# A fp32 decoder trunk in three-product arithmetic: the order of the first norm's halves, the place of the last closing's turn, and the order of products in the merge projection

## The chip, the cores and the metric

One core of a Trainium2 chip runs the whole program. The metric is device time in microseconds, the median over timed runs. The engines are TensorE (PE, with its weight loads as PEld), VectorE (DVE), ScalarE (ACT), GpSimd (POOL) and SyncE (SP), whose queue issues the large loads.

## The reference, cut to what matters

Two layers, x of 256 tokens by 1024 features, everything in float32:

```python
for l in range(2):
    h = rmsnorm(x, norm_mix[l])
    q_a, k_a, v_a, q_b, k_b, v_b, z, xbc, dt_raw = split_cols(h @ w_in[l], IN_SIZES)
    y_a = swa_sink_attention(rope(q_a), rope(k_a), v_a, sinks)      # 8 heads of 64
    y_b = moba_attention(q_b, k_b, v_b)                              # 8 heads of 64
    y_c = ssd_mixer(z, xbc, dt_raw, ...)                             # 16 heads of 64, chunks of 128
    g_a, g_b, g_c = split(sigmoid(h @ w_gate[l] + b_gate[l]), 3)
    merged = g_a * (y_a @ w_br_swa[l]) + g_b * (y_b @ w_br_moba[l]) + g_c * (y_c @ w_br_ssd[l])
    x = x + merged @ w_mix_out[l]
    x = x + cross_attention(rmsnorm(x, norm_cross[l]), rmsnorm(mem, norm_mem[l]))
    x = x + square(relu(rmsnorm(x, norm_mlp[l]) @ w_up[l])) @ w_down[l]
return rmsnorm(x, final_norm)
```

## The kernel before, in words

**Units.** The weights of a layer are cut into 93 units of up to 1 MB, numbered by the order in which PE takes them. A unit is 4 row tiles by 512 columns ("B": tokens on the output's partitions, two token tiles one after the other) or 8 row tiles by 256 columns ("A": output columns on the partitions, two column tiles m = 0 and 1). Each weight is used as a rounded high part and a low part, `w_hi` and `w_lo`, and each activation likewise; a product is three matmuls: high by high, high by low, low by high. An A unit is 48 matmuls, 24 in each half m. Units 0 and 1 are the first projection (`qa`), 2 is `qkb`, 3 to 5 are `kva`, 6 is `xbc`, 33 to 36 the last four gate units, 37 to 40 the third branch's projection `branch_c` (`w_br_ssd`; `U_BRC` is 37), 41 to 44 `mix` (`w_mix_out`; `U_MIX` is 41), 45 to 48 `kx`.

**The ring.** `raw`, `w_hi` and `w_lo` have three slots. SP loads unit u into `raw` when the low part of unit u - 3 has been made. ACT makes the high part (`hi`, line 751) after the load has landed and PE is through with unit u - 3; DVE makes the low part (`lo`, line 1468), and PE waits for that. ACT and DVE run `hi(u + 3)` and `lo(u + 3)` in the part of their program that belongs to unit u, in order with all else that they do.

**The order of other work.** All engines walk the same list of units; what belongs to a unit's slot stands in each engine's loop body. On PE, "inner" work is put between the two halves of a unit (`inner`), "outer" work behind the unit. SP's queue has one more stop: ahead of the load of unit 38 it waits for the end of the last of the third branch's products (`ssd_y`, 4), issues the 1 MB load of `mem` into the memory that `z_sb` used, and then the load of unit 38 (lines 589 to 591, and 641).

**The closings.** A closing ends a part of an attention or scan branch: DVE makes `y_tok` (line 1848 is the last step for the scan), PE turns it by four transposes into a PSUM bank (`close_turn`, line 1335), ACT reads the bank and makes the high part (`close_hi_part`, line 902), DVE reads it and makes the low part (`close_lo_part`, line 1862). There are eight, 0 to 7. Closing 7 holds the second token tile of group 1, that is the row tiles k = 4 to 7 of the operand `y_ssd` of `branch_c`. Its DVE part belongs to unit 34. Inner closings have `close_hi_part` at the head of ACT's body for their slot; outer ones have it a few lines further down in the body, but still ahead of `evacuate` and `hi(l, u + 3)`. Both kinds have it at their own slot:

```python
for i in INNER_CLOSINGS:
    if u == TURN_SLOT[i]:
        close_hi_part(l, i)
...
if u + RING < NU and w["kind"] != "xbc":
    hi(l, u + RING)
```

**The first norm.** `norm` keys ("norm", 0, b) are four PSUM banks: b = 2 t + u for token tile t and the k half of unit u. PE turns `h_tok` into them (`norm0_turn`, line 1189), ACT makes the high part of the activation (`norm_gain_hi`, line 781), DVE the low part (line 1489). Units 0 and 1 are multiplied in `opening`. Their weights are cut into halves of 1024 columns of a slot (`hi_half` line 760, `lo_half` line 1605), with signals of their own.

**Merged.** The merged activation is made in four parts (`mg_hi` by ACT, line 856, `mg_lo` by DVE, line 1759). Between units 41 and 42 PE does 16 transposes of `mem` (`norm_turn`, line 1208).

**The xs turn.** In slot 23 PE turns xs group 1 into the banks 7 (token tile 0) and 4 (token tile 1); DVE reads each with two products (`xs_tokens`, lines 1893 and 1895). Bank 7 is the one that PE's next turn of probabilities (line 1294) goes to.

Of the kernel before, what the change touches and what calls it, by code (L numbers as in the profile page):

```python
# [39 lines left out]
TT = SEQ // P  # L40
# [106 lines left out]
U_GATE, U_BRA, U_BRB, U_BRC, U_MIX = (first_of(k) for k in ("gate", "branch_a", "branch_b", "branch_c", "mix"))  # L147
# [44 lines left out]
CLOSINGS = [(3, 0, 0, 0), (7, 0, 1, 0), (11, 1, 0, 0), (15, 1, 1, 0),  # L192
            (17, 2, 0, 0), (19, 2, 0, 1), (21, 2, 1, 0), (23, 2, 1, 1)]
CLOSE_SLOT = [job_slot(c[0]) + 2 for c in CLOSINGS]
INNER_CLOSINGS, OUTER_CLOSINGS = (0, 1, 2, 6), (3, 4, 5, 7)
TURN_SLOT = [s + (3 if i == 1 else 2 if i in INNER_CLOSINGS else 1) for i, s in enumerate(CLOSE_SLOT)]

INNER_SLOTS = (ACS_SLOT, BTOK_SLOT, CB_SLOT) + XS_SLOTS + tuple(TURN_SLOT[i] for i in INNER_CLOSINGS)
# [120 lines left out]
def trunk(nc, a, out):  # L319
    ctx = ExitStack()  # L320
    with ctx:
# [113 lines left out]
        def sem(name):  # L435
            return ctx.enter_context(nc.semaphore(name))
# [66 lines left out]
        pool_steps = Signal(sem("pool_steps"), 9)  # L503
        sq_fin, ms_fin, rstd_fin = sem("sq_fin"), sem("ms_fin"), sem("rstd_fin")
        gain_ready, gained, fin_upper = sem("gain_ready"), sem("gained"), sem("fin_upper")

        def bank(key):
            return psum[:, BANK_OF[key][0], :]
# [10 lines left out]
        def is_read(l, key):  # L519

            b, k = BANK_OF[key]
            return bank_free[b], l * BANK_USES[b] + (k + 2)
# [214 lines left out]
        def _(act):  # L737
# [185 lines left out]
            def start(l):  # L923

                x_left(act, l, 0)
                square(0, 0, x_sb, sq_done.sem)
                if l == 0:
                    x_left(act, l, 1)
                    square(0, 1, x_sb, sq_done.sem)
                hi_half(l, 0, 0)  # L930
                if l == 0:
                    act.wait_ge(mix_cols, 1)
                    norm_gain_hi(l, 0, (0,))
                    hi_half(l, 0, 1)
                    norm_gain_hi(l, 0, (1,))
                    hi_half(l, 1, 0)
                    norm_gain_hi(l, 0, (2,))
                    hi_half(l, 1, 1)
                    norm_gain_hi(l, 0, (3,))
                    hi(l, 2)  # L940
                else:
                    hi_half(l, 0, 1)
                    norm_gain_hi(l, 0, (0, 1))
                    hi_half(l, 1, 0)
                    hi_half(l, 1, 1)
                    x_left(act, l, 1)
                    square(0, 1, x_sb, sq_done.sem)
                    hi(l, 2)
                    norm_gain_hi(l, 0, (2, 3))
# [97 lines left out]
        def _(pe):  # L1047
# [19 lines left out]
            def operand_ready(l, u):  # L1067

                w = UNITS[u]
                act, j = w["act"], w["index"]  # L1070
                if act == "relu":
                    pe.wait_ge(*relu_l.at(l, 2 * (j // 2) + 2))
                elif act == "merged":
                    pe.wait_ge(*mg_lo.at(l, 2 if w["first"] else 4))
                elif u > 0 and UNITS[u - 1]["act"] == act and (u != U_CO + 1):
                    return
                elif act == "mem":
                    wait_read(pe, l, [("norm", 1, b) for b in range(4)])
                elif act in ("h", "hq", "hf"):
                    return  # L1080
                elif act == "o":
                    wait_read(pe, l, [("xvalues", h) for h in ((0, 1) if w["first"] else (2, 3))])
                else:
                    pe.wait_ge(*is_read(l, ("closeT", {"y_swa": 1, "y_moba": 3, "y_ssd": 7}[act])))

            def unit(l, u, tiles=range(TT)):
                w, slot = UNITS[u], u % RING
# [30 lines left out]
                elif w["orient"] == "A":  # L1118
                    for m in range(n // P):
                        if m == 1:  # L1120
                            inner(l, u)
                        dst = bank(unit_banks(u, w)[m // 2])[:, (m % 2) * SEQ:(m % 2 + 1) * SEQ]
                        for k in range(kt):
                            if turned and m == 0 and k % 2 == 0:
                                pe.wait_ge(*is_read(l, ("norm", turned, k // 2)))
                            cs = slice(m * P, (m + 1) * P)
                            pe.matmul(dst, m_hi[:, k, cs], a_hi[:, k, :], start=k == 0, stop=False)  # L1127
                            pe.matmul(dst, m_hi[:, k, cs], a_lo[:, k, :], start=False, stop=False)  # L1128
                            ins = pe.matmul(dst, m_lo[:, k, cs], a_hi[:, k, :], start=False, stop=k == kt - 1)  # L1129
                else:  # L1130
                    for t in tiles:
                        if t == 1:
                            inner(l, u)
                        dst = bank(unit_bank(u, t))[:, 0:n]
                        for k in range(kt):
                            first, last = w["first"] and k == 0, w["last"] and k == kt - 1
                            ts = slice(t * P, (t + 1) * P)
                            pe.matmul(dst, a_hi[:, k0 + k, ts], m_hi[:, k, :], start=first, stop=False)  # L1138
                            pe.matmul(dst, a_hi[:, k0 + k, ts], m_lo[:, k, :], start=False, stop=False)  # L1139
                            ins = pe.matmul(dst, a_lo[:, k0 + k, ts], m_hi[:, k, :], start=False, stop=last)  # L1140
                if TT - 1 in tiles:
                    ins.then_inc(unit_done.sem, 1)
                elif u in GROUP_ENDS:
# [2 lines left out]
            def opening(l, u, t):  # L1146

                dst, m_hi, m_lo = (bank(unit_bank(u, t)), *(w[:, u, :].rearrange("p (k n) -> p k n", n=512)
                                                            for w in (w_hi, w_lo)))
                ts = slice(t * P, (t + 1) * P)  # L1150
                if u == 0:
                    pe.wait_ge(*is_free(l, unit_bank(u, t)))
                pe.wait_ge(*norm_hi.at(l, 2 * t + u + 1))
                for ks in ((0, 1), (2, 3)) if t == 0 else (range(4),):
                    last = ks[-1] == 3
                    if last:
                        pe.wait_ge(*hi_ready.at(l, u + 1))
                    else:
                        pe.wait_ge(*(hi_first, hi_second)[u].at(l, 1))
                    for k in ks:  # L1160
                        pe.matmul(dst, act_hi[:, 4 * u + k, ts], m_hi[:, k, :], start=u == 0 and k == 0, stop=False)
                    if last:
                        wait_lo(pe, l, u)
                    else:
                        pe.wait_ge(*(lo_first, lo_second)[u].at(l, 1))
                    for k in ks:
                        pe.matmul(dst, act_hi[:, 4 * u + k, ts], m_lo[:, k, :], start=False, stop=False)
                    pe.wait_ge(*is_read(l, ("norm", 0, 2 * t + u)))
                    for k in ks:
                        ins = pe.matmul(dst, act_lo[:, 4 * u + k, ts], m_hi[:, k, :], start=False,  # L1170
                                        stop=u == 1 and k == 3)
                    if (u, t) == (l > 0, 0) and not last:
                        norm0_turn(l, 1, (0,))
                if (u, t) == (l > 0, 0):
                    norm0_turn(l, 1, (1,))
                if t == TT - 1:
                    ins.then_inc(unit_done.sem, 1)
                elif u == 1:
                    ins.then_inc(tile0_done.sem, 1)
# [191 lines left out]
            for l in range(DEPTH):  # L1371
                for u in range(NU):
                    if u in GROUPS:
                        if u == U_QA:
                            if l == 0:
                                norm0_turn(l, 0)
                            for i, t in ((0, 0), (0, 1), (1, 0), (1, 1)) if l == 0 else ((0, 0), (1, 0), (0, 1), (1, 1)):
                                if (l, i, t) == (0, 1, 1):
                                    rows_turn()
                                opening(l, i, t)  # L1380
                            continue
# [49 lines left out]
        def _(dve):  # L1431
# [48 lines left out]
            def norm_gain_lo(l, n, banks=range(4)):  # L1480
                dst_hi, dst_lo = (hm_hi, hm_lo) if n == 1 else (act_hi, act_lo)
                for b in banks:
                    key = ("norm", n, b)
                    dve.wait_ge(*norm_hi.at(l, 4 * n + b + 1))
                    if n == 0:
                        for i in range(4):
                            k, ts = 4 * (b % 2) + i, slice((b // 2) * P, (b // 2 + 1) * P)
# [103 lines left out]
            def start(l):  # L1591
# [16 lines left out]
                if l == 0:  # L1608
                    scaled(0)
                    scaled(1)  # L1610
                    lo_half(0, 0)
                    norm_gain_lo(l, 0, (0,))
                    lo_half(0, 1)
                    norm_gain_lo(l, 0, (1,))
                    lo_half(1, 0)
                    norm_gain_lo(l, 0, (2,))
                    lo_half(1, 1)
                    norm_gain_lo(l, 0, (3,))
                    lo(l, 2)
# [263 lines left out]
            def xs_tokens(l, g):  # L1883
# [2 lines left out]
                    dve.wait_ge(*values_done.at(l, 8))  # L1886
                for t in range(TT):
                    dve.wait_ge(*is_full(l, ("xs", g, t)))
                for t in (1, 0):
                    key = ("xs", g, t)  # L1890
                    src = bank(key).rearrange("p (h d) -> p h d", d=HD)
                    hs = slice(8 * g, 8 * g + 8)
# [97 lines left out]
```

## Time and profile before

| | |
|---|---|
| median of 3 runs | 1189.03 us (1189.0 to 1190.13) |
| the profiled execution, its time / its span | 1189.82 us / 1188.1 us |
| PE busy | 1170.8 us (99%) |
| PEld busy | 1051.2 us (88%) |
| DVE busy | 777.1 us (65%) |
| ACT busy | 572.9 us (48%) |
| POOL busy | 60.6 us (5%) |
| mean DMA rate | 169 GB/s |
| mean granted TensorE clock | 0.997 |

The span is from the first to the last instruction. PE's busy time is a union of modelled spans: a matmul is drawn 0.28 or 0.39 us long while its successor starts 0.12 or 0.23 us after it, so that an idle time in a row is some 0.15 us shorter than the true pause between two starts. A row of the timeline has the start and the duration in microseconds, then engine, line, operation, output and inputs, shape, count of merged instructions, and in brackets the engine's idle time before it and what ended that.

### The profile page before, as it was taken

The page shows a single profiled execution, that of the slowest core. Times are in us where ns is not written, and L with a number is a line of the kernel's source. Part 1 is how long each engine was busy: PE and PEld are TensorE (multiplying, and loading weights), DVE is VectorE, ACT ScalarE, POOL GpSimd, SP SyncE. Part 2 cuts the span into 40 slices and gives each one's busy share as a digit, 9 for nine tenths or more (in the row PEclk, how much of TensorE's full clock was granted, in tenths as well). Part 3 has the DMA queues.
Part 4 walks back from the last instruction along what each step waited for, and adds up shares of the span by engine and source line. Part 5 has one row for each costly group of instructions (what it writes and reads, how often), then busy time and mean ns, then how long its engine had stood idle before and what let it go on. Part 6 is the DMA issues. An engine that isn't in the chain of part 4 may idle for free.

```text
span 1188.1 us, 18386 instructions
## 1 busy us (share of the span) xinstructions
PE 1170.8 (99%) x7523; PEld 1051.2 (88%) x7523; DVE 777.1 (65%) x1174; ACT 572.9 (48%) x811; POOL 60.6 (5%) x93
## 2 busy tenths in 40 slices
PE   8999999999999999999999999999999999999997
PEld 7988899999998888888889888999989988888886
DVE  6877756877545475665578777579675455766565
ACT  5655444545455355444355545453465444544443
POOL 1000002300000000000000000033000000000000
PEclk9999999999999999999999999999999999999999
DMA  7743425655654455655456444355656443665661
GB/s 238 232 142 125 160 81 178 217 164 181 214 175 142 142 177 189 200 178 191 163 153 205 142 143 139 103 173 190 213 177 209 146 142 107 228 197 177 195 207 41
DMA packets 156428, 201.31 MB, mean 169 GB/s; under 512 B 7168, under 2 KB 111928, under 8 KB 156344
## 3 DMA queue, kind: packets, MB, share of 16 engines
q1 hardware_dynamic: 155616, 199.58, 52.2%
q8 instruction: 60, 0.98, 0.3%
q10 hardware_dynamic: 728, 0.55, 0.1%
q14 instruction: 24, 0.20, 0.0%
HBM read 199.04 MB, written 1.08 MB: 168 GB/s over the span
## 4 chain that ended last, share of the span: by engine, by line
PE 83%; DVE 5%; issue 4%; DMA 4%; ACT 3%; POOL 1%; SPq 0%; DVEq 0%; POOLq 0%; ACTq 0%
PE psum L1138 10%; PE psum L1115 10%; PE psum L1140 10%; PE psum L1139 10%; PE psum L1127 9%; PE psum L1128 9%; PE psum L1129 9%; PE psum L1116 5%; ACT w_hi L751 2%; DMA raw<-in_w_br_ssd_dram 2%; PE psum L1322 2%; PE psum L1283 1%; PE psum L1294 1%; DVE w_lo L1468 1%; PE psum L1344 1%
## 5 line engine op out<-in xcount | busy, mean ns | idle before, releaser
L1468 DVE TENSOR_TENSOR w_lo<-raw,w_hi 128x2048 fp32r<-128x2048 f32 (+1 forms) x182 | 408.9, 2250 | 214.8 <-ACT w_hi L751 214.1
L751 ACT ACTIVATE w_hi<-raw 128x2048 fp32r<-128x2048 f32 (+1 forms) x182 | 341.7, 1879 | 151.7 <-PE psum L1140 109.7
L1127 PE MATMUL psum<-act_both,w_hi 128*128 128x256 f32 x832 | 241.0, 290 | 0.0
L1128 PE MATMUL psum<-act_both,w_hi 128*128 128x256 f32 x832 | 235.2, 283 | 0.0
L1129 PE MATMUL psum<-act_both,w_lo 128*128 128x256 f32 x832 | 235.2, 283 | 0.0
L1115 PE MATMUL psum<-act_both,w_hi 128*128 128x512 f32 x512 | 181.8, 399 | 0.0
L1127 PEld LDWEIGHTS psum<-act_both,w_hi 128*128 128x128 f32 x832 | 159.3, 191 | 1.1 <-issue 0.5
L1128 PEld LDWEIGHTS psum<-act_both,w_hi 128*128 128x128 f32 x832 | 159.4, 192 | 0.6 <-issue 0.5
L1129 PEld LDWEIGHTS psum<-act_both,w_lo 128*128 128x128 f32 x832 | 159.2, 191 | 0.0
L1116 PE MATMUL psum<-act_both,w_lo 128*128 128x256 f32 x512 | 143.7, 281 | 0.0
L1115 PEld LDWEIGHTS psum<-act_both,w_hi 128*128 128x128 f32 x512 | 96.1, 188 | 24.3 <-DVE act_both L1497 0.7
L1138 PE MATMUL psum<-w_hi,relu_hi 128*128 128x512 f32 x256 | 100.1, 391 | 0.0
L1140 PE MATMUL psum<-w_hi,relu_lo 128*128 128x512 f32 x256 | 99.8, 390 | 0.0
L1139 PE MATMUL psum<-w_lo,relu_hi 128*128 128x512 f32 x256 | 99.7, 389 | 0.0
L1116 PEld LDWEIGHTS psum<-act_both,w_lo 128*128 128x128 f32 x512 | 96.7, 189 | 0.5
L1138 PE MATMUL psum<-w_hi,act_both 128*128 128x512 f32 (+1 forms) x192 | 73.2, 381 | 1.0 <-DVE act_both L1759 1.0
L1140 PE MATMUL psum<-w_hi,act_both 128*128 128x512 f32 (+1 forms) x192 | 71.8, 374 | 0.0
L1139 PE MATMUL psum<-w_lo,act_both 128*128 128x512 f32 (+1 forms) x192 | 71.6, 373 | 0.0
L814 ACT ACTIVATE tmp<-psum 128x256 f32<-128x256 f32 x64 | 21.1, 382 | 92.7 <-PE psum L1116 92.7
L794 ACT ACTIVATE pT_sb<-psum 128x256 f32<-128x256 f32 (+1 forms) x32 | 15.7, 490 | 89.2 <-PE psum L1294 89.2
L1140 PEld LDWEIGHTS psum<-w_hi,relu_lo 128*128 128x128 f32 x256 | 48.0, 188 | 10.4
L1138 PEld LDWEIGHTS psum<-w_hi,relu_hi 128*128 128x128 f32 x256 | 48.0, 188 | 10.2
(262 smaller groups left out, 1962.5 us busy)
## 6 DMA issues: line engine op xcount, KB each, us to landing
raw<-in_w_in_dram SPq DMA_DIRECT2D x34, 1024.0 KB, 5.2
raw<-in_w_up_dram SPq DMA_DIRECT2D x32, 1024.0 KB, 5.3
raw<-in_w_down_dram SPq DMA_DIRECT2D x32, 1024.0 KB, 5.0
raw<-in_w_gate_dram SPq DMA_DIRECT2D x24, 1024.0 KB, 7.1
raw<-in_w_ckv_dram SPq DMA_DIRECT2D x16, 1024.0 KB, 5.3
raw<-in_w_br_ssd_dram SPq DMA_DIRECT2D x8, 1024.0 KB, 10.0
raw<-in_w_mix_out_dram SPq DMA_DIRECT2D x8, 1024.0 KB, 5.5
raw<-in_w_cq_dram SPq DMA_DIRECT2D x8, 1024.0 KB, 5.2
```

What stands on the lines that cost most here:

```text
L751: act.activation(w_hi[:, slot, 0:n], raw[:, slot, 0:n], ACT.Copy).then_inc(hi_ready.sem, 1)
L814: ins = act.activation(tmp[:, j % 2, m * SEQ:(m + 1) * SEQ], bank((u, m))[:, SEQ:2 * SEQ], ACT.Copy)
L1115: pe.matmul(dst, m_hi[:, k, cs], act_both[:, :, k, :], start=k == 0, stop=False)
L1116: ins = pe.matmul(dst[:, 0:SEQ], m_lo[:, k, cs], a_hi[:, k, :], start=False, stop=k == kt - 1)
L1127: pe.matmul(dst, m_hi[:, k, cs], a_hi[:, k, :], start=k == 0, stop=False)
L1128: pe.matmul(dst, m_hi[:, k, cs], a_lo[:, k, :], start=False, stop=False)
L1129: ins = pe.matmul(dst, m_lo[:, k, cs], a_hi[:, k, :], start=False, stop=k == kt - 1)
L1138: pe.matmul(dst, a_hi[:, k0 + k, ts], m_hi[:, k, :], start=first, stop=False)
L1139: pe.matmul(dst, a_hi[:, k0 + k, ts], m_lo[:, k, :], start=False, stop=False)
L1140: ins = pe.matmul(dst, a_lo[:, k0 + k, ts], m_hi[:, k, :], start=False, stop=last)
L1322: ins = pe.matmul(bank(key)[:, hs], pT_sb[:, n % 2, c:c + P], v, start=k == 0, stop=k == t)
L1468: dve.tensor_tensor(w_lo[:, slot, 0:n], raw[:, slot, 0:n], w_hi[:, slot, 0:n].bitcast(F32), ALU.subtract).then_inc(lo_ready.sem, 1)
```

## The change

Five edits:

1. In layer 0, the high part of the first half of unit 0 is made by DVE (a copy) and no longer by ACT; the halves and banks of the first norm are taken in the order bank 0, 2, 1, 3 by ACT and DVE, and PE turns bank 0 and 2 ahead of the first products and bank 1 and 3 behind the first token tile's products of unit 0.
2. In `opening` (both layers) the products of the second half are put in another order, with all low-activation products behind one wait; for the first token tile the products of the last quarter of `w_lo` come last. In layer 1 the turn of the second token tile's first bank moves behind ten of the twelve products of unit 1.
3. Closing 7 is turned inside unit 36, between its halves, and no longer behind unit 35. `branch_c` starts after closing 6 has been read, and PE waits for closing 7 ahead of k = 4 of unit 37's first half.
4. In unit 42 the eight products of each token tile that need only the high part of merged come first, and the wait for its low part stands behind them.
5. `xs_tokens` reads token tile 0 first for group 1.

```diff
-INNER_CLOSINGS, OUTER_CLOSINGS = (0, 1, 2, 6), (3, 4, 5, 7)
+INNER_CLOSINGS, OUTER_CLOSINGS = (0, 1, 2, 6, 7), (3, 4, 5)
 TURN_SLOT = [s + (3 if i == 1 else 2 if i in INNER_CLOSINGS else 1) for i, s in enumerate(CLOSE_SLOT)]
...
+        def norm_place(l, n, b):
+            return 4 * n + ((0, 2, 1, 3)[b] if (l, n) == (0, 0) else b) + 1
...
-                hi_half(l, 0, 0)
                 if l == 0:
                     act.wait_ge(mix_cols, 1)
                     norm_gain_hi(l, 0, (0,))
                     hi_half(l, 0, 1)
+                    norm_gain_hi(l, 0, (2,))
+                    hi_half(l, 1, 0)
                     norm_gain_hi(l, 0, (1,))
-                    hi_half(l, 1, 0)
-                    norm_gain_hi(l, 0, (2,))
                     hi_half(l, 1, 1)
                     norm_gain_hi(l, 0, (3,))
                     hi(l, 2)
                 else:
+                    hi_half(l, 0, 0)
...
                 elif act == "merged":
-                    pe.wait_ge(*mg_lo.at(l, 2 if w["first"] else 4))
+                    if w["first"]:
+                        pe.wait_ge(*mg_lo.at(l, 2))
+                    else:
+                        pe.wait_ge(*mg_hi.at(l, 4))
...
-                    pe.wait_ge(*is_read(l, ("closeT", {"y_swa": 1, "y_moba": 3, "y_ssd": 7}[act])))
+                    pe.wait_ge(*is_read(l, ("closeT", {"y_swa": 1, "y_moba": 3, "y_ssd": 6}[act])))
...
+                            if (u, m, k) == (U_BRC, 0, 4):
+                                pe.wait_ge(*is_read(l, ("closeT", 7)))
...
-                            ins = pe.matmul(dst, a_lo[:, k0 + k, ts], m_hi[:, k, :], start=False, stop=last)
+                            if u != U_MIX + 1:
+                                ins = pe.matmul(dst, a_lo[:, k0 + k, ts], m_hi[:, k, :], start=False, stop=last)
+                        for k in range(kt) if u == U_MIX + 1 else ():
+                            pe.wait_ge(*mg_lo.at(l, 4))
+                            ins = pe.matmul(dst, a_lo[:, k0 + k, ts], m_hi[:, k, :], start=False, stop=k == kt - 1)
...
+                pe.wait_ge(*(hi_first, hi_second)[u].at(l, 1))
+                products(act_hi, m_hi, (0, 1), first=True)
+                pe.wait_ge(*(lo_first, lo_second)[u].at(l, 1))
+                products(act_hi, m_lo, (0, 1))
+                pe.wait_ge(*hi_ready.at(l, u + 1))
+                products(act_hi, m_hi, (2, 3))
+                if t == 1:
+                    wait_lo(pe, l, u)
+                    products(act_hi, m_lo, (2, 3))
+                pe.wait_ge(*is_read(l, ("norm", 0, 2 * t + u)))
+                ins = products(act_lo, m_hi, (0, 1, 2, 3), last=t == 1)
+                if (l > 0, u, t) == (True, 1, 0):
+                    norm0_turn(l, 1, (0,))
+                if t == 0:
+                    wait_lo(pe, l, u)
+                    ins = products(act_hi, m_lo, (2, 3), last=True)
+                if (l > 0, u, t) == (True, 1, 0):
+                    norm0_turn(l, 1, (1,))
+                if (l, u, t) == (0, 0, 0):
+                    for i in range(TT):
+                        norm0_turn(l, i, (1,))
...
-                                norm0_turn(l, 0)
+                                for t in range(TT):
+                                    norm0_turn(l, t, (0,))
...
+                    dve.wait_ge(raw_first, 16)
+                    dve.tensor_copy(w_hi[:, 0, 0:1024], raw[:, 0, 0:1024]).then_inc(hi_first.sem, 1)
                     lo_half(0, 0)
                     norm_gain_lo(l, 0, (0,))
                     lo_half(0, 1)
+                    norm_gain_lo(l, 0, (2,))
+                    lo_half(1, 0)
                     norm_gain_lo(l, 0, (1,))
-                    lo_half(1, 0)
-                    norm_gain_lo(l, 0, (2,))
                     lo_half(1, 1)
                     norm_gain_lo(l, 0, (3,))
                     lo(l, 2)
...
-                for t in (1, 0):
+                for t in ((1, 0), (0, 1))[g]:
                     key = ("xs", g, t)
```

## Rows read from the trace of the kernel before

**Rows 1.** Waits of PE: line, what it waited for, total us, times, longest.
```profile
PE psum L1335 <- DVE y_tok L1848: 2.3, 2, 1.4
PE psum L1189 <- DVE h_tok L1595: 1.6, 2, 1.2
PE psum L1294 <- DVE xd_sb L1895: 1.1, 2, 0.5
PE psum L1138 <- DVE act_both L1759: 1.0, 2, 0.7
```
**Rows 2.** Timeline of layer 0's third branch, SP's queue.
```profile
252.90 0.37 SPq L590 DMA_DIRECT2D mem_sb<-in_mem_dram  x1
253.32 1.09 SPq L641 DMA_DIRECT2D raw<-in_w_br_ssd_dram  x2
```
**Rows 3.** Timeline of the same stretch, ACT.
```profile
255.79 1.14 ACT L902 ACTIVATE yc_hi<-psum,cols 128x128 fp32r<-128x128 f32 x4 [5.56 <-PE psum L1335]
...
262.25 1.92 ACT L751 ACTIVATE w_hi<-raw 128x2048 fp32r<-128x2048 f32 x1 [4.59 <-DMA raw<-in_w_br_ssd_dram]
```
**Rows 4.** Timeline of the same stretch, DVE.
```profile
257.16 1.12 DVE L1862 SCALAR_TENSOR_TENSOR yc_lo<-psum,cols,yc_hi 128x128 fp32r<-128x128 f32 x4
264.19 2.29 DVE L1468 TENSOR_TENSOR w_lo<-raw,w_hi 128x2048 fp32r<-128x2048 f32 x1 [5.92 <-ACT w_hi L751]
```
**Rows 5.** Timeline of the same stretch, PE: first matmuls of units 37 and 38.
```profile
261.34 0.28 PE L1127 MATMUL psum<-yc_hi,w_hi 128*128 128x256 f32 x1
...
267.10 0.28 PE L1127 MATMUL psum<-yc_hi,w_hi 128*128 128x256 f32 x1
```
**Rows 6.** Layer 1: ACT and DVE on unit 38, PE's first matmuls of 37 and 38.
```profile
848.16 1.92 ACT L751 ACTIVATE w_hi<-raw 128x2048 fp32r<-128x2048 f32 x1 [4.90 <-DMA raw<-in_w_br_ssd_dram]
...
850.11 2.29 DVE L1468 TENSOR_TENSOR w_lo<-raw,w_hi 128x2048 fp32r<-128x2048 f32 x1 [6.23 <-ACT w_hi L751]
...
846.93 0.28 PE L1127 MATMUL psum<-yc_hi,w_hi 128*128 128x256 f32 x1
...
852.70 0.28 PE L1127 MATMUL psum<-yc_hi,w_hi 128*128 128x256 f32 x1
```
**Rows 7.** Windows: us, busy (x) of PE, PEld, DVE, ACT, POOL, PEclk, DMA share, GB/s.
```profile
10.00:11.00 1.00, 0.25 (x1) 0.28 (x2) 1.00 (x2) 1.00 (x4) 0.00 (x0) 0.76 1.04 401
13.00:14.00 1.00, 1.00 (x5) 0.77 (x4) 1.00 (x5) 0.57 (x1) 0.00 (x0) 0.53 1.09 346
838.00:842.00 4.00, 2.65 (x23) 2.44 (x22) 3.02 (x5) 0.61 (x3) 0.74 (x2) 1.00 0.61 168
```
**Rows 8.** Timeline of the start: DVE's scaling and first low half, PE's first product.
```profile
8.08 0.75 DVE L1595 TENSOR_SCALAR h_tok<-x_sb,rstd 128x1024 f32<-128x1024 f32 x1 [0.72 <-POOL rstd L692]
9.66 1.23 DVE L1605 TENSOR_TENSOR w_lo<-raw,w_hi 128x1024 fp32r<-128x1024 f32 x1 [0.82 <-ACT w_hi L760]
...
10.75 0.77 PE L1161 MATMUL psum<-w_hi,act_both 128*128 128x512 f32 x1 [2.24 <-ACT act_both L781]
```
**Rows 9.** Timeline: DVE's low part of unit 5, PE's first matmul of unit 5.
```profile
32.68 1.01 DVE L1468 TENSOR_TENSOR w_lo<-raw,w_hi 128x816 fp32r<-128x816 f32 x1 [0.54 <-DVE mark_sb L1694]
...
33.95 0.29 PE L1138 MATMUL psum<-w_hi,act_both 128*128 128x272 f32 x1
```
**Rows 10.** Timeline of DVE: last xs read of slot 23; a scan job's decays.
```profile
168.82 0.68 DVE L1895 TENSOR_TENSOR xd_sb<-psum,cols 128x512 f32<-128x512 f32 x1
...
219.39 1.42 DVE L1784 SCALAR_TENSOR_TENSOR s_sb<-pT_sb,acs,mask_ssd 128x128 f32<-128x128 f32 x4 [0.66 <-PE psum L1314]
```
**Rows 11.** Timeline of layer 1's opening: ACT's bank 2, PE's first product of it.
```profile
602.60 1.14 ACT L781 ACTIVATE act_both<-psum,cols 128x128 fp32r<-128x128 f32 x4 [1.45 <-PE psum L1189]
...
604.14 0.48 PE L1161 MATMUL psum<-w_hi,act_both 128*128 128x512 f32 x1
```
**Rows 12.** Timeline of layer 1: ACT's last part of merged, unit 42's first matmul.
```profile
876.45 0.63 ACT L856 ACTIVATE act_both<-mg_sb 128x512 fp32r<-128x512 f32 x1 [5.01 <-DVE mg_sb L1735]
...
878.02 0.47 PE L1138 MATMUL psum<-w_hi,act_both 128*128 128x512 f32 x1 [0.66 <-DVE act_both L1759]
```

More of the change, by code:

```diff
@@ L1152, in opening @@
                     pe.wait_ge(*is_free(l, unit_bank(u, t)))
[L1153 to L1159, printed above, removed]
-                    for k in ks:
[L1161 to L1173, printed above, removed]
@@ L1174, in opening, with products @@
-                if (u, t) == (l > 0, 0):
+                pe.wait_ge(*norm_hi.at(l, norm_place(l, 0, 2 * t + u)))
+                def products(x, w, ks, first=False, last=False):
+                    for k in ks:
+                        ins = pe.matmul(dst, x[:, 4 * u + k, ts], w[:, k, :], start=first and u == 0 and k == 0,
+                                        stop=last and u == 1 and k == ks[-1])
+                    return ins
+                pe.wait_ge(*(hi_first, hi_second)[u].at(l, 1))
@@ L1483, in norm_gain_lo @@
                     key = ("norm", n, b)
-                    dve.wait_ge(*norm_hi.at(l, 4 * n + b + 1))
+                    dve.wait_ge(*norm_hi.at(l, norm_place(l, n, b)))
                     if n == 0:
```

## The prediction

> **What bounds the kernel now.** PE is busy for 1170.8 of 1188.1 us, so I read PE's own waits first: whatever stops PE for a microsecond costs one, and little else costs anything. Four of them are what this change is about [rows 1]: the turn of closing 7 waits for `y_tok` (2.3 us in two, the longer 1.4, so 0.9 in layer 0 and 1.4 in layer 1), layer 1's opening waits for the scaled second token tile (1.2), the turn of probabilities for a bank that DVE reads (1.1 in two), and unit 42 for the low part of merged (1.0 in two). A fifth is the start, where PE's first product waits 2.24 us [rows 8]. Together they are under 9 us, 0.7% of the kernel. Then I followed, for each moved step, what stands ahead of it in the queue of the engine that does it. That is where this change is decided. The reader should see one row above all: ACT's high part of unit 38 starts at 262.25, after 4.59 us of idle time that ended with a landing [rows 3]. It is so late because SP issues `mem` at 252.90, when the scan's last product is done, and unit 38's load only behind that, at 253.32 [rows 2]. Layer 1 repeats it: 848.16, after 4.90 us [rows 6].
>
> **Part 3, the closing.** What it removes: PE no longer stops behind unit 35, 0.9 and 1.4 us. The turn itself (four transposes) moves to the middle of unit 36 and costs the same there.
>
> What it moves with it: the slot of closing 7 goes from 35 to 36 on all engines. In ACT's program `close_hi_part` of closing 7 stood ahead of `hi` of unit 38 (slot 35) and ran at 255.79 [rows 3]. Now it belongs to slot 36, and `hi` of unit 38 is ahead of it. ACT stands in that `hi` until the load lands at 262.25. DVE's order turns round in the same way: `close_lo_part` ran at 257.16, and now the low part of unit 38, at 264.19, is ahead of it [rows 4].
>
> Layer 0, step by step. ACT: 262.25 + 1.92 = 264.17, then the closing's four activations, 1.14 [rows 3], end at about 265.3. DVE: low part of unit 38 from 264.19 for 2.29, then the closing's low part, 1.12, started some 0.09 before the other is drawn to end: 264.19 + 2.29 - 0.09 + 1.12 = 267.5 [rows 4]. So closing 7 has been read at 267.5. With 0.06 for the signal PE goes on at 267.57. Where is PE by then? Unit 37 began at 261.34 [rows 5]; without the pause of 0.9 (1.06 from start to start) it begins at 260.3, does the twelve matmuls of k = 0 to 3 in 1.44 us (48 matmuls take 267.10 - 261.34 = 5.76, so 0.12 each) and stops at 261.7. It is idle for 5.8 us. Then 36 matmuls, 4.32 us: unit 38 begins at 271.9 in place of 267.10, 4.8 us later.
>
> Layer 1 [rows 6]: 850.11 + 2.29 - 0.09 + 1.12 + 0.06 = 853.5, and 4.32 more is 857.8 in place of 852.70, 5.1 us later. PE is idle for about 6.8 us. Both: +9.9 us. The pause that was removed is in this difference already, and the rest of it is paid in full, since PE goes on without a pause behind it.
>
> The clock. In the first 11 us PE was idle for 2.24 us [rows 8], and the granted clock fell within that: 0.76 in 10 to 11 us, and it is 0.53 in 13 to 14, so it came back to full only at about 13.5 [rows 7]. That is the level of 1.2 GHz in place of 2.4 for about 2.8 us of PE's work, half of it lost, 1.4 us. The pause of 1.4 us in layer 1 left the clock at 1.00 [rows 7]. A pause of 5.8 or 6.8 us is well beyond the one that lowered it, so I take 1.4 us for each layer: +2.8. Its bounds are 0 and some 4 in all.
>
> Behind ACT's waiting instruction stand the evacuation of gate unit 36 and the high part of unit 39; behind DVE's the low part of unit 39. They come at about 266 and 268 to 270, while PE wants unit 39 at 279: hidden. Unit 38's weights, that had 0.6 us to spare (264.19 + 2.29 = 266.48 against 267.10 [rows 4, 5]), have several now.
>
> **Part 1, the start.** ACT's first high half goes to DVE, so ACT makes bank 0's activation at once and PE's first product starts when DVE's copy is done. The copy has no row. Its nearest rows of that size are 0.75 us (scaling by one scalar, 128x1024) and 1.23 (two tensors) [rows 8]; I take 0.75. DVE is through with the scaling at 8.83, so the copy ends at 9.6 and the low half follows at 9.6, as it did at 9.66. With 1.23, everything on DVE is 0.4 later. "VectorE: DVE Perf Modes" in the Trainium skill, section on the perf-mode tier table, has an fp32 copy within SBUF and an operation with a scalar in the same tier, twice the rate of two tensors; by it the sum would stay as it is, and by the 1.23 it would be 0.35 us more. The scaling's row agrees, and no row here shows the copy.
>
> PE then begins its products some 1.1 us earlier than 10.75, and without a long pause, perhaps at full clock. But that isn't what sets the time further on. The low part of unit 5 is made by DVE from 32.68 to 33.69, behind a long chain (the low parts of units 2 and 3, the sine tables, the rotation) that starts no more than 0.1 us earlier, and PE takes unit 5 at 33.95 [rows 9]. So PE can be 0.26 + 0.1 earlier behind it: -0.35. Bounds: 0 (slow copy) and -1.4 (the chain doesn't hold PE).
>
> **Part 2, layer 1's opening.** The turn for which PE waited 1.2 us [rows 1] stands four products (0.9 us) later, and that wait nearly goes. But bank 2's high part ends at 602.60 + 1.14 = 603.74, since it depends on the same scaled tile, and PE needs it at what was 604.14 [rows 11]. The wait moves there: -0.3.
>
> **Part 4, merged.** Its last high part ends at 877.08 [rows 12], ahead of the end of the transposes (878.02 less the idle 0.66 is 877.36), and the eight products in front (1.8 us) cover the low part, which released PE at 878.02. The whole wait goes: 1.0 [rows 1] drawn, 1.3 from start to start, less what a boundary costs: -1.2 in both layers. Bounds -1.0 and -1.3.
>
> **Part 5, xs.** Bank 7 was the second to be read, until 169.5 [rows 10]. Read first, it is free two products of 0.68 earlier, which is more than the wait of 0.5 [rows 1]: -1.3 in both layers with the modelled ends. The cost is nothing: DVE does the same four reads.
>
> **Do gains ahead of the stall count?** Only if the scan's last product, which starts the loads, comes earlier too. DVE's chain towards it waits for PE at 219.39 (0.66 us idle) [rows 10], so it follows PE and I count them. If it doesn't, some 1.9 of the gains are lost.
>
> **Sum.** +9.9 + 2.8 - 0.35 - 0.3 - 1.2 - 1.3 = +9.55 us. The profiled execution has a span of 1188.1 and a time of 1189.8, 0.8 above the median of the runs, 1189.0. The median becomes 1189.0 + 9.6 = 1198.6 us, 0.8% slower. A measurement of this kernel can tell about 0.2% (2.4 us) from no change.
>
> **The rivals.**
>
> *The stall comes, but the clock stays high or returns at once.* Without the 2.8 the time is 1195.8. For it: PE is still at 1.00 through a pause of 1.4 us. Against it: the fall within a pause of 2.24. Chance 0.2.
>
> *The stall is hidden and the change does what it says (the other side).* Units 37 and on take closing 7 without a wait if ACT gets to it in time, that is if unit 38's load lands by about 256.4: closing 7 would have to be read by 261.7, 5.85 us ahead of 267.57, and the landing as much ahead of 262.25. Then only the gains are left, -3.15, and of the closing's pauses what unit 38's weights allow: 0.6 in layer 0 and 0.3 in layer 1 (852.40 against 852.70 [rows 6]). That gives -4.05: 1185.0. The load is issued at 253.32 and would have 3 us in place of 8.9, so it takes another order of loads than this one. Chance 0.07.
>
> *The stall is longer than worked out:* the gains ahead of it are lost (+1.9), or the clock stays low for longer in both layers (+1.2): 1200 to 1201.7. Chance 0.13.
>
> *The forecast:* 0.6. Its own range is 1197 to 1200.
>
> **Range and chances.** From the forecast the range reaches down to the rival with a high clock, 1195.8, with 1.3 below it for part 1's bound of -1.4, and up to 1201.5. 1194.5 to 1201.5 leaves out the hidden stall and a little on both sides. Faster by over 0.2%: 0.07. Within: 0.03, a stall of some 3 us in one layer. Slower: 0.90.
>
> **What would show it.** In the changed kernel's trace ACT's line 902 for closing 7 stands right behind the line 751 that waits for `w_br_ssd`, near 264 and 850 (shifted by what went before). PE has two pauses of 5 to 7 us inside unit 37, ended by DVE's `yc_lo`, each followed by some 3 us at half the clock, and none at the closing's turn. Line 1294 no longer waits for `xd_sb`, nor unit 42 for `act_both`. PE's first product is at about 9.7, and unit 5 at about 33.6. The prediction is wrong if ACT gets to closing 7 ahead of unit 38's high part, or if unit 38's load lands some 6 us earlier than it did.

## The result, and the profile after

The changed kernel takes 1198.71 us (median of 6 runs, 1197.51 to 1200.59) against 1189.58 us of the kernel before in the same measurement (6 runs, 1188.64 to 1190.76): a ratio of 1.0076, 95% interval 1.0063 to 1.0089. The profiled execution has a time of 1199.23 us and a span of 1197.5 us, 9.4 more than before. PE is busy for 1175.2 us (98%), DVE 778.1, ACT 571.9; the mean granted clock is 0.994.

PE's own waits in the changed kernel, from the view of waits (line, what it waited for, total us, times, longest), to be read against [rows 1]:

```profile
PE psum L1135 <- DVE yc_lo L1882: 10.5, 2, 5.4
PE psum L1053 <- DMA rows<-in_norm_mix_dram: 2.8, 1, 2.8
PE psum L1206 <- DVE h_tok L1613: 0.8, 2, 0.5
PE psum L1168 <- DVE w_lo L1623: 0.5, 1, 0.5
PE psum L1168 <- issue: 0.4, 1, 0.4
```

Of the four waits of [rows 1] that the change is about three are gone (nothing for `y_tok`, `xd_sb` or merged's `act_both`) and the fourth, for `h_tok`, is shorter: 0.8 us in place of 1.6. In their place stands one new wait of twice 5 us. The timeline of layer 0's third branch, SP's queue, then ACT, then DVE, then PE, shows where it is from ([rows 2] to [rows 5] are its counterparts):

```profile
251.54 0.37 SPq L593 DMA_DIRECT2D mem_sb<-in_mem_dram  x1
251.95 5.09 SPq L644 DMA_DIRECT2D raw<-in_w_br_ssd_dram  x3
...
260.01 1.91 ACT L754 ACTIVATE w_hi<-raw 128x2048 fp32r<-128x2048 f32 x1 [6.53 <-DMA raw<-in_w_br_ssd_dram]
261.82 1.12 ACT L905 ACTIVATE yc_hi<-psum,cols 128x128 fp32r<-128x128 f32 x4
...
261.95 2.29 DVE L1486 TENSOR_TENSOR w_lo<-raw,w_hi 128x2048 fp32r<-128x2048 f32 x1 [6.07 <-ACT w_hi L754]
264.16 1.12 DVE L1882 SCALAR_TENSOR_TENSOR yc_lo<-psum,cols,yc_hi 128x128 fp32r<-128x128 f32 x4
...
259.95 0.28 PE L1137 MATMUL psum<-yc_hi,w_lo 128*128 128x256 f32 x1
265.33 0.58 PE L1135 MATMUL psum<-yc_hi,w_hi 128*128 128x256 f32 x1 [5.11 <-DVE yc_lo L1882]
265.71 0.41 PE L1136 MATMUL psum<-yc_lo,w_hi 128*128 128x256 f32 x1
265.92 0.41 PE L1137 MATMUL psum<-yc_hi,w_lo 128*128 128x256 f32 x1
```

The reader should follow the chain by its numbers: ACT stands 6.53 us until unit 38's load lands at 260.0, makes its high part, and only then the closing's; DVE does the same with its two. PE, behind its twelfth matmul of unit 37 (the one at 259.95), waits for the last of these, `yc_lo`. Then its matmuls start 0.21 us apart where before they were 0.12 apart. The windows of that stretch say why (us, busy (x) of PE, PEld, DVE, ACT, POOL, granted clock, DMA share, GB/s):

```profile
262.00:264.00 2.00, 0.00 (x0) 0.00 (x0) 2.00 (x1) 2.00 (x7) 0.00 (x0) 1.00 1.10 349
264.00:266.00 2.00, 0.67 (x3) 0.67 (x4) 1.77 (x6) 1.48 (x1) 0.00 (x0) 0.57 0.72 162
266.00:268.00 2.00, 2.00 (x11) 2.00 (x11) 1.80 (x1) 0.00 (x0) 0.00 (x0) 0.50 0.99 367
268.00:270.00 2.00, 2.00 (x12) 2.00 (x11) 0.00 (x0) 0.00 (x0) 0.00 (x0) 0.50 0.82 193
270.00:272.00 2.00, 2.00 (x14) 2.00 (x14) 0.00 (x0) 0.00 (x0) 0.00 (x0) 0.72 1.04 404
272.00:274.00 2.00, 2.00 (x19) 2.00 (x18) 1.38 (x2) 0.07 (x1) 0.00 (x0) 1.00 0.21 71
```

The granted clock falls to half, the level of 1.2 GHz, while PE is idle, and it is still there for 5.8 us in which PE works without a pause (265.33 to 271.1: the 0.72 of 270 to 272 is 1.1 us at half). Layer 1, timeline of ACT, DVE and PE, is the same picture (compare [rows 6]):

```profile
850.82 1.91 ACT L754 ACTIVATE w_hi<-raw 128x2048 fp32r<-128x2048 f32 x1 [6.78 <-DMA raw<-in_w_br_ssd_dram]
852.64 1.13 ACT L905 ACTIVATE yc_hi<-psum,cols 128x128 fp32r<-128x128 f32 x4
...
854.97 1.12 DVE L1882 SCALAR_TENSOR_TENSOR yc_lo<-psum,cols,yc_hi 128x128 fp32r<-128x128 f32 x4
...
856.15 0.58 PE L1135 MATMUL psum<-yc_hi,w_hi 128*128 128x256 f32 x1 [5.36 <-DVE yc_lo L1882]
```

The start of the changed kernel, timeline of DVE, PE and ACT (compare [rows 8]):

```profile
9.15 0.69 DVE L1630 CAST w_hi<-raw 128x1024 fp32r<-128x1024 f32 x1
...
9.99 0.70 PE L1168 MATMUL psum<-w_hi,act_both 128*128 128x512 f32 x2 [0.22 <-DVE w_hi L1630]
...
23.47 0.89 ACT L754 ACTIVATE w_hi<-raw 128x816 fp32r<-128x816 f32 x1 [3.45 <-PE psum L1168]
24.37 1.28 ACT L957 ACT_TABLE_LOAD   x1
```

To see where the 9.4 us of span come from I compared, unit by unit, when PE starts its first matmul in the two traces (after less before, us):

| PE's start of | layer 0 | layer 1 |
|---|---|---|
| first unit (layer 1: unit 0, second token tile) | -0.76 | +4.57 |
| unit 3 (layer 1: unit 24) | -0.95 | +3.83 |
| unit 24 | -1.60 | |
| unit 37 | -2.71 | +2.26 |
| unit 38 | +5.18 | +10.26 |
| unit 42 | +4.59 | +9.36 |

Between the starts of the units 37 and 38 lie +7.9 us in layer 0 and +8.0 us in layer 1. The other steps of the table are gains, but for +0.3 near unit 64, between the two columns.

### The profile page after: what moved, and what is told of

It is laid out like the page before. It is cut to its first block, busy times and chain, and to the rows that moved or that the text cites. A ratio compares the mean times of both kernels' runs of the same rounds, so it can differ in the third digit from the quotient of the medians.

```text
span 1197.5 us, 18386 instructions
## 1 busy us (share of the span) xinstructions
PE 1175.2 (98%) x7523; PEld 1055.1 (88%) x7523; DVE 778.1 (65%) x1175; ACT 571.9 (48%) x810; POOL 60.6 (5%) x93
## 4 chain that ended last, share of the span: by engine, by line
PE 88%; DVE 4%; DMA 3%; issue 2%; ACT 1%; POOL 1%; SPq 0%; POOLq 0%; DVEq 0%; ACTq 0%
PE psum L1146 10%; PE psum L1135 10%; PE psum L1147 10%; PE psum L1136 10%; PE psum L1137 10%; PE psum L1121 10%; PE psum L1149 10%; PE psum L1122 5%; PE psum L1339 2%; PE psum L1168 1%; PE psum L1300 1%; DMA raw<-in_w_br_ssd_dram 1%; DVE w_lo L1486 1%; DMA raw<-in_w_gate_dram 1%; PE psum L1311 1%
## 5 line engine op out<-in xcount | busy, mean ns | idle before, releaser
L1146 PE MATMUL psum<-w_hi,act_both 128*128 128x512 f32 (+1 forms) x192 | 73.3, 382 | 0.1
L1149 PE MATMUL psum<-w_hi,act_both 128*128 128x512 f32 (+1 forms) x176 | 65.5, 372 | 0.0
```

## The experiments

The kernels were timed in three groups, each beside the kernel before on the same chip; rows with the same "before", which is the median of its runs, are one group. Each "us" is the median of 5 executions, for the small parts (parts 1 and 2, part 4, part 5) of 11, and for the products' filler of 8. One of those 8 took 6626.93 us, for which I have no explanation; the other seven lie between 1192.64 and 1195.65 us and have a median of 1192.97.

| kernel | us | before | ratio, 95% interval |
|---|---|---|---|
| closing 7 as before | 1185.87 | 1190.2 | 0.9965, 0.9952 to 0.9979 |
| part 3 alone | 1200.28 | 1190.2 | 1.0091, 1.0079 to 1.0104 |
| `mem` one unit later | 1183.10 | 1190.2 | 0.9945, 0.9933 to 0.9958 |
| closing served first | 1183.69 | 1190.2 | 0.9953, 0.9940 to 0.9965 |
| pause filled, products | 1193.28 | 1189.97 | 1.0030, 1.0019 to 1.0040 |
| pause filled, transposes | 1194.48 | 1189.97 | 1.0041, 1.0028 to 1.0054 |
| parts 1 and 2 alone | 1188.63 | 1189.97 | 0.9988, 0.9979 to 0.9997 |
| both cures | 1182.68 | 1189.97 | 0.9941, 0.9928 to 0.9953 |
| closing 7 as before, `mem` later | 1185.65 | 1190.09 | 0.9964, 0.9952 to 0.9977 |
| part 4 alone | 1189.07 | 1190.09 | 0.9992, 0.9983 to 1.0001 |
| part 5 alone | 1189.07 | 1190.09 | 0.9989, 0.9980 to 0.9998 |

**Part 3 undone, and part 3 alone.** Is the closing the whole loss? The first kernel is the changed one with the closing put back:

```diff
-INNER_CLOSINGS, OUTER_CLOSINGS = (0, 1, 2, 6, 7), (3, 4, 5)
+INNER_CLOSINGS, OUTER_CLOSINGS = (0, 1, 2, 6), (3, 4, 5, 7)
...
-                            if (u, m, k) == (U_BRC, 0, 4):
-                                pe.wait_ge(*is_read(l, ("closeT", 7)))
```

(and `y_ssd` waits for closing 7 again). 

> The changed kernel with closing 7 put back behind unit 35 (part 3 undone), the other four parts kept. Theory (the place of closing 7 in the queues of ScalarE and VectorE costs all of the loss): by the shifts of PE's unit starts between the two traces, part 3 is worth +13.2 us (unit 36 to 38: -1.60 to +5.18 in layer 0, +3.83 to +10.26 in layer 1), so this kernel is at 1198.7 - 13.2 = 1185.5 us, 0.34% under the kernel before, with pauses of 0.9 and 1.4 us at the closing's turn and none in unit 37. Rival (another part shares in the loss, such as a landing or a bank that comes late once PE is earlier): it stays above 1188.

It took 1185.87 us, as expected. So in the changed kernel part 3 costs 1198.7 - 1185.9 = 12.8 us (13.2 by the two ratios, which take out the difference between the groups), and the other four parts are worth 4.2 (2.5 to 5.7).

The second is the kernel before with part 3 and nothing else. 

> The kernel before with part 3 alone. Theory: 1189.3 + 13.2 = 1202.5 us, and two pauses of PE of 5 to 6 us in unit 37, each with nearly 6 us at half the clock behind it. Rival (the size of the pause depends on the gains ahead of it, which bring PE to unit 37 earlier but not the load): the pauses are 1.6 to 2.3 us shorter, and the time is 1198 to 1200.

It took 1200.28: 2.2 us under the theory and just above the rival's 1198 to 1200, so the 13.2 us don't carry over. Its PE has the pauses (9.8 us in two for `yc_lo`), and from the start of unit 35 to that of unit 38 it falls back by 5.8 us in layer 0 and 5.5 in layer 1, 11.3 in all. The rival's reason covers a third of the difference: from start to start the pauses are 5.03 and 5.13 us, together 0.6 less than in the changed kernel. The rest is the clock: the 36 matmuls behind the pause took 6.24 and 6.25 us, where the changed kernel's took 6.95 and 6.81. At unit 42 this kernel gains 0.6 and 0.9 us without part 4: the pause itself gives ACT and DVE the time to finish merged. So the gain at that place in the changed kernel isn't part 4's.

**Two cures of the new wait.** If the loss is the order "the half that waits for a load, then the half that PE waits for", either of two edits must take it away. One sends unit 38's load ahead of `mem`:

```diff
-                    if u == U_BRC + 1:
+                    if u == U_BRC + 2:
                         sp.wait_ge(*ssd_y.at(l, 4))
```

> The changed kernel, with the wait for the scan's last product and the load of mem ahead of unit 39's load in SyncE's queue in place of unit 38's. Unit 38's load is issued some 6 us earlier. Theory (the late landing of unit 38 is what holds closing 7 back): ScalarE's high part of unit 38 is done before the closing's turn, no pause in unit 37, no fall of the clock, and the two pauses at the closing's turn are gone too: 1185.5 - 2.6 = 1182.9 us. Rival (the closing is late by its own four steps, whatever the load does): a pause of 1 us or more stays in unit 37 and the time is above 1185.5.

The other leaves the loads alone and lets ACT and DVE serve closing 7 in slot 35, ahead of unit 38's halves:

```diff
                     for i in INNER_CLOSINGS:
-                        if u == TURN_SLOT[i]:
+                        if u == TURN_SLOT[i] - (i == 7):
                             close_hi_part(l, i)
```

(the same for `close_lo_part`). 

> The changed kernel, with ScalarE's and VectorE's parts of closing 7 put back into slot 35, ahead of their parts of unit 38; PE's turn stays inside unit 36, and the loads are as in the changed kernel. Theory (order in the two queues): no pause in unit 37, since the closing is read at about 257.5 in layer 0, but unit 38's weights are ready only a few tenths of a us before PE wants them in the kernel before, so that of the 2.6 us of the closing's pauses only 0.6 + 0.3 come back, or up to 2 if the load lands as early as it did in the changed kernel's trace: 1183.5 to 1184.6 us. Rival (the landing itself, not the order, is what counts): PE still waits 5 us or more in each layer and the time is above 1195.

They took 1183.10 and 1183.69, both as expected. The timeline of the first, SP and ACT:

```profile
246.14 0.37 SPq L644 DMA_DIRECT2D raw<-in_w_br_ssd_dram  x1
252.16 0.37 SPq L593 DMA_DIRECT2D mem_sb<-in_mem_dram  x1
...
254.00 1.92 ACT L754 ACTIVATE w_hi<-raw 128x2048 fp32r<-128x2048 f32 x1
256.59 1.14 ACT L905 ACTIVATE yc_hi<-psum,cols 128x128 fp32r<-128x128 f32 x4 [0.67 <-PE psum L1352]
```

and of the second, ACT:

```profile
255.54 1.14 ACT L905 ACTIVATE yc_hi<-psum,cols 128x128 fp32r<-128x128 f32 x4 [6.96 <-PE psum L1352]
256.55 0.86 ACT L848 ACTIVATE g_sb<-psum,half 128x256 f32<-128x256 f32 x2
259.53 1.92 ACT L754 ACTIVATE w_hi<-raw 128x2048 fp32r<-128x2048 f32 x1 [2.12 <-DMA raw<-in_w_br_ssd_dram]
```

The reader should see the releaser in brackets: `close_hi_part` now waits for PE's turn, that is for its own input, and no load stands in front of it, in the one because the load came 6 us earlier, in the other because its reader comes behind. In neither does PE wait in unit 37. The second also settles that the load's lateness alone does nothing: there it still lands late (259.5), ACT waits 2.12 us for it, and PE doesn't wait.

**What the pause costs beside its length.** The pause was 5.26 and 5.52 us from start to start, but the loss between units 37 and 38 was 7.9 and 8.0. To take the clock away from it and leave the wait, the changed kernel got idle work in the pause:

```diff
                             if (u, m, k) == (U_BRC, 0, 4):
+                                pe.wait_ge(*is_read(l, ("values", 22)))
+                                for _ in range(19):
+                                    pe.matmul(psum[:, OB_, :], yc_hi[:, 0, 0:P], w_lo[:, u % RING, 0:512], start=True, stop=True)
                                 pe.wait_ge(*is_read(l, ("closeT", 7)))
```

> The changed kernel with 19 idle products of 512 columns put into the pause of unit 37, behind the matmuls of its A product and before its wait for the low halves; their results go to a bank that is overwritten and are read by nobody. A first product took 0.22 us, so they fill some 4.2 of the 5.1 and 5.4 us of pause. Theory (the pause costs twice: its own length, and 2.6 us a layer of half clock behind it): the pause itself stays, the clock stays at 1.00 through 264 to 272 us, and the kernel takes 1198.7 - 2 x 2.6 = 1193.5 us. Rival (the half clock behind the pause has another cause, such as the load or the burst of work on ScalarE and VectorE when it lands): the stretch of half clock stays and the time is 1198 to 1199.5.

The other filler has 38 times `pe.transpose(psum[:, OB_, 0:P], ident[:], ident[:])` there. 

> The same with 38 transposes of the identity (128 x 128) in place of the products, 0.11 us each, so 4.2 us again. At the start of the kernel before, stretches in which TensorE ran turns alone stood beside a granted clock that later fell. The Trainium skill (TensorE) has transposes not counted as busy for the clock. If so: the stretch of half clock behind the pause stays and the time is 1198 to 1199.5, as in the changed kernel. If transposes hold the clock as products do: 1193.5, as the other filler.

They took 1193.28 and 1194.48: both fillers give the clock back. The windows of the products' kernel (columns as above):

```profile
264.00:266.00 2.00, 1.05 (x8) 0.92 (x8) 1.77 (x5) 1.22 (x1) 0.00 (x0) 1.00 0.54 100
266.00:268.00 2.00, 2.00 (x19) 2.00 (x18) 1.55 (x1) 0.00 (x0) 0.00 (x0) 1.00 1.03 398
```

and of the transposes' kernel:

```profile
264.00:266.00 2.00, 1.53 (x12) 1.53 (x13) 1.77 (x3) 0.61 (x1) 0.00 (x0) 1.00 0.78 192
266.00:268.00 2.00, 2.00 (x19) 2.00 (x18) 0.94 (x1) 0.00 (x0) 0.00 (x0) 1.00 0.96 375
```

PE's timeline in the same kernel:

```profile
259.51 4.31 PE L1135 MATMUL psum<-ident 128*128 128x128 f32 x38
264.47 0.39 PE L1138 MATMUL psum<-yc_hi,w_hi 128*128 128x256 f32 x1 [0.65 <-DVE yc_lo L1885]
```

In 266 to 268 us PE does 19 matmuls where it did 11. The wait ends when it did, within 1 us (265.08 with the products, 265.33 without), so what the filler saves is nearly all the clock: 1198.7 - 1193.3 = 5.4 us, against 2.6 + 2.5 worked out below. The transposes' row says more: PE ran nothing but transposes for 4.3 us, and the clock was at 1.00 behind them. "TensorE: Matmul & The Clock Gate" of the Trainium skill ("Part 4: PE-mode transpose") has transposes in TensorE's transpose mode not count as busy in the same way; by that the stretch of half clock would have stayed, and these fp32 transposes don't bear it out in either layer. The trace draws them as MATMUL and doesn't tell whether that mode was on. The 1.2 us between the two fillers isn't explained; their intervals overlap.

**Both cures.** 

> The changed kernel with both cures of the new wait: the last closing's half placed ahead of the half that waits for the load, and the small load ahead of the two large ones sent one unit later. Each alone took the pause away (1183.7 and 1183.1). Theory: there is nothing left to gain from the second, so 1182.8 to 1183.8, and no wait of PE for the low closing half. Rival: the two add up or disturb each other at the next load, outside of 1182.3 to 1184.3.

1182.68, that is 0.4 us less than with the later `mem` alone and 1.0 less than with the closing served first alone, neither of which is told apart from nothing. It is the fastest version, 0.9941 of the kernel before.

**Is part 3 worth anything once cured?** The changed kernel with the closing as before and `mem` sent later. 

> The changed kernel with part 3 undone and the small load sent one unit later: what the cure is worth without the closing inside the unit. Theory (the load mattered only because the closing's low half stood behind it): with the closing between the units nothing waits for that load, so 1185.9, as with part 3 undone alone; then part 3 with the cure is worth 1185.9 - 1183.1 = 2.8. Rival (the earlier load is itself worth something): 1183 to 1184.5, and part 3 would be worth nothing even cured.

1185.65, a ratio of 0.9964 where the same kernel with `mem` in its old place has 0.9965, so nothing came from the load by itself. With the cure part 3 is worth 1185.65 - 1183.1 = 2.6 us, or 1185.87 - 1183.10 = 2.8 between two kernels of one group, whose runs don't overlap. That is the wait for `y_tok` that it was to remove (2.7 us in two in the kernel with closing 7 as before).

**The small parts.** Parts 1 and 2 alone. 

> The kernel before with parts 1 and 2 alone: the order of the first norm's banks and weight halves. The profile of the changed kernel had PE's units of layer 0 0.9 us early by unit 5 and layer 1's opening another 0.3 us early. Theory (sines end earlier because the table load no longer waits behind the half): 1189.6 - 1.2 = 1188.4, with the shift of 0.9 us seen again at unit 5. Rival (the early sines were chance of one execution): the shift is 0.3 to 0.4 and the time 1188.9 to 1189.3.

Part 4 alone. 

> The kernel before with part 4 alone (the high products of merged ahead of its low ones). Theory: 0.5 and 0.8 us at unit 42 of the two layers, as it showed between the two kernels without the pause, so 1189.8 - 1.3 = 1188.5. Rival (what part 4 saves comes back at the next wait of PE): 1189.5 to 1190.

Part 5 alone. 

> The kernel before with part 5 alone (the xs banks in the order of their turns). Theory: 0.7 us a layer at the values, so 1189.8 - 1.4 = 1188.4, with the shift seen before unit 36. Rival (it comes back by unit 38, as the halves of y_ssd then wait for the weights): 1189.5 to 1190.

1188.63, 1189.07 and 1189.07. Worked out from the ratios, that is -1.4 us (-2.5 to -0.4), -1.0 (-2.0 to +0.1) and -1.3 (-2.4 to -0.2): each agrees with its theory, but the intervals are too wide to shut out the rivals, and part 4's takes in zero. The three add up to -3.7 against the -4.2 of the kernel that has them all. In the trace part 4 is -0.53 and -0.81 us at unit 42, as expected. Part 5 is -0.72 between unit 1 and unit 24 of layer 0, but later in that layer its profile gives all of it back, as its rival said: +0.3 at unit 36 and +0.5 more at unit 42. In layer 1 the -0.73 of unit 24 is kept. The profile of parts 1 and 2 gives back most, -0.71 at unit 3 and -0.16 at unit 42, and its shift at unit 5, -0.64, lies between its theory's 0.9 and its rival's 0.3 to 0.4. Both keep the old closing. The times don't show that much loss, so I leave the size open.

## Why the prediction was right, by its own steps

It said 1198.6 us; it is 1198.71. The mechanism of part 3 was right in each link: ACT's closing behind the `hi` that waits for `w_br_ssd`, DVE's behind the low part, two pauses inside unit 37 ended by `yc_lo`, none at the closing's turn, and the two cures bear it out. But several sizes were off, and the sum is close because they cancel: that it comes within 0.1 us is luck.

**Part 3, the pause: too long in the sum.** The step was "ACT stands in that `hi` until the load lands", with the landing as far behind PE's work as before. From there the chain ran as worked out: 5.3 us from the start of `hi` of unit 38 to PE's resumption in both layers (260.01 to 265.33, 850.82 to 856.15; predicted 262.25 to 267.57). But in layer 0 the load was issued 1.37 us earlier (251.95 in place of 253.32) and landed 0.9 us sooner behind its issue: 8.1 in place of 8.9. In layer 1 it was 8.0 in place of 9.2. PE itself stopped only 1.6 us earlier in layer 0, so the pauses were 5.26 and 5.52 us, in place of 5.9 and some 6.8. The sooner landing came with the change and wasn't chance: with closing 7 behind unit 35 and `mem` ahead of unit 38 all ten landings in five traces, read from the start of `hi`, are 8.8 to 9.5 us behind the issue, and with the closing's turn inside unit 36 all ten in five others 7.6 to 8.4. The DMA packets show one thing that goes with it. In each of the first ten a load of 16 KB of instructions starts 5.7 to 6.2 us behind the issue, in the midst of unit 38's load, and takes 1.1 to 1.2 us; in the other ten it starts ahead of the issue, or none starts in the 4 us ahead of it. The DMA view of the kernel before, from the issue to the landing in layer 0, has it as queue 8 (packets, MB, share of 16 engines):

```profile
q1 hardware_dynamic: 2027, 2.83, 97.2%
q8 instruction: 1, 0.02, 0.8%
```

Nothing moved that load alone, so that it is the cause isn't shown.

**Part 3, the clock: half of what it is.** I took 1.4 us a layer from the start of the kernel, as half of 2.8 us. That was misread by a little: 0.53 in 13 to 14 us puts the return at 13.9, not 13.5, so 3.2 us and 1.6 [rows 7]. Measured: 36 matmuls took 272.28 - 265.33 = 6.95 us in layer 0 and 6.81 in layer 1 in place of 4.32, so +2.6 and +2.5. The fillers confirm it: 5.4 us. My upper bound, "some 4 in all", was too low as well. What failed is "I take 1.4 us for each layer", the length of the low stretch carried over from the start. Behind PE's resumption it lasted 5.8 and 5.5 us here, and the start doesn't fix it either: in the profile of part 4 alone, with the old start, it is at 0.58 in 10 to 11 us and still at 0.51 in 16 to 17. Nor is it one price for one pause: in the kernel with part 3 alone the same matmuls cost +1.9 us in each layer.

**Together** part 3 moved PE by -1.60 to +5.18 = +6.8 us in layer 0 and +3.83 to +10.26 = +6.4 in layer 1, +13.2 in all; predicted +12.7. The pauses, without the clock, came out 1.8 us under their term of 9.9, and the clock 2.3 over its 2.8.

**Part 1: -0.35 predicted at unit 5, -0.87 there in this profile (-0.95 at unit 3).** The copy on DVE took 0.69 us (estimate 0.75), and the first product came at 9.99 (predicted 9.7; the scaling that the copy stands behind was itself 0.2 us later here). The step that failed is "that chain starts no more than 0.1 us earlier". ACT's sine tables stand behind `hi` of unit 4, and that waits for PE's products of the opening, which came 1.2 us earlier: `hi` ran at 23.47 and the table load at 24.37, where before, in ACT's timeline, they ran at 24.68 and 25.59:

```profile
24.68 0.89 ACT L751 ACTIVATE w_hi<-raw 128x816 fp32r<-128x816 f32 x1 [4.89 <-PE psum L1170]
25.59 1.28 ACT L954 ACT_TABLE_LOAD   x1
```

So the chain that I took for DVE's own has PE in it. The bound of -1.4 held it: over the profiles of the kernels with the new start the shift at unit 3 was from -0.3 to -1.5.

**Part 2: -0.3 predicted, -0.29 measured** (+4.86 to +4.57), with the wait split: 0.31 us at the turn and 0.38 ahead of the products of bank 2.

**Part 4: -1.2 predicted, -1.5 measured at the place, but not earned by it.** In the kernel with part 3 alone the wait went without it, by 0.6 and 0.9. Without the pause part 4 is worth 1.3 in the trace, as the step said.

**Part 5: -1.3 predicted**, -1.4 in this profile (0.72 in each layer). "Do gains ahead of the stall count?": they did. `mem` was issued 1.36 us earlier, with PE 1.6 us early at unit 24.

**The rivals.** A clock that stays high or returns at once would have given 1195.8; the filled kernels show what that is like, 1193.3, and the unfilled one isn't it. The hidden stall took another order of loads, as the rival said, and one line made it; its 1185.0 was 2 us too slow, since with the load early unit 38's weights set no limit and the closing's whole pause was gained. The longer stall was right in that the clock stayed low for longer, and wrong in the total.

## What to carry to other kernels

Moving a small step one slot later is moving it behind everything in that slot on each in-order queue: look for an instruction there that waits for a transfer, since the step inherits that wait. Such a wait is cured on either side, by the order of the queue that reads or of the queue that loads, and both were one line here. Price a pause of a saturated PE at its length plus what the clock takes behind it, and give the second a wide range: here pauses of 5.0 to 5.5 us cost 1.9 to 2.6 us on top, and 5.3 cost 7.9 in all.

## What the runs showed of the hardware beyond that

- After a pause of 5.3 to 5.5 us the granted clock was low before PE resumed (0.57 in 264 to 266 us, 0.70 in 854 to 856) and it came back only 5.8 and 5.5 us behind PE's resumption, with PE working without a pause. With idle work in 4.3 to 4.5 us of the same wait it never fell, in either layer, whether that work was products or fp32 transposes.
- At the start the low clock comes and goes by execution. The four profiles with the old start (the kernel before, parts 3, 4 and 5 alone) all have a stretch below 1.00 between 10 and 18 us. Of nine with the new start only two have one (`mem` later, with and without the closing). So part of what part 1 gives may be a better chance of a full clock there; thirteen profiles don't settle it, and one can't price it.
- A 1 MB load that shared the DMA engines with three others landed 8.8 to 9.5 us behind its issue in ten cases and 7.6 to 8.4 in ten others, in both layers. What parts the two groups is the place of the closing's turn, and with it that of a 16 KB load of instructions. A sum that takes a landing from the kernel before has about 1 us of play, and the change itself can shift it.
